# Attention, output projection and expert routing in three groups of three tiles, two of them inside the gather phase

## What is computed

```python
def fox_block(q, k, v, cq, ck, qpos, kpos):
    logits = jnp.einsum('bqhd,bkhd->bhqk', q, k).astype(F32) * (FOX_HD ** -0.5)
    logits = logits + (cq.transpose(0, 2, 1)[..., :, None] - ck.transpose(0, 2, 1)[..., None, :])
    logits = jnp.where((kpos[None, :] <= qpos[:, None])[None, None], logits, -jnp.inf)
    p = jax.nn.softmax(logits, axis=-1)
    return jnp.einsum('bhqk,bkhd->bqhd', p.astype(v.dtype), v)

def peer_tokens(x, wq, keys, u, v):
    q = jnp.einsum('nd,dc->nc', x, wq).reshape(n, PEER_HEADS, 2, PEER_HALF)
    s1 = jnp.einsum('nhd,hkd->nhk', q[:, :, 0], keys[0]).astype(F32)
    s2 = jnp.einsum('nhd,hkd->nhk', q[:, :, 1], keys[1]).astype(F32)
    v1, i1 = lax.top_k(s1, PEER_TOPK)
    v2, i2 = lax.top_k(s2, PEER_TOPK)
    cand = (v1[..., :, None] + v2[..., None, :]).reshape(n, PEER_HEADS, TOPK * TOPK)
    cv, ci = lax.top_k(cand, PEER_TOPK)          # and e: the expert numbers
    g = jax.nn.softmax(cv, axis=-1)
    act = jax.nn.gelu(jnp.einsum('nd,nhkd->nhk', x, u[e]).astype(F32))
    return jnp.einsum('nhk,nhkd->nd', g * act, v[e])

x = x + combine(ro, rg, fo, ret_out_g, fox_out_g, w_out, x.dtype)
x = x + peer(rms_norm(x, norm2_g), peer_wq, peer_keys, peer_u, peer_v)
```

## Time and profile before

| | us |
|---|---|
| median of three runs (4229.17 to 4239.43) | 4231.19 |
| the profiled execution | 4230.94 |
| its span, first to last instruction | 4229.1 |
| first attention scores | 690.00 |
| first gather issued | 1255.99 |
| first dot product | 1261.99 |
| VectorE, TensorE, ScalarE, POOL busy | 2474.3, 2507.5, 447.5, 1406.0 |
| mean DMA rate over the span | 305 GB/s |

### The profile page before, as it was taken

The page is one execution under the profiler, slowest core; times in us unless marked ns, Lnnn a source line. Parts: engine busy times, 40 slices in busy tenths (PEclk is TensorE's granted clock), DMA queues, the critical chain, the costliest instruction groups (busy, mean ns, idle before and its releaser), DMA issues.

```text
span 4229.1 us, 34501 instructions
## 1 busy us (share of the span) xinstructions
PE 2507.5 (59%) x11938; PEld 1040.8 (25%) x11938; DVE 2474.3 (59%) x6323; ACT 447.5 (11%) x1214; POOL 1406.0 (33%) x1276
## 2 busy tenths in 40 slices
PE   7998998998976336435435435534634634633333
PEld 3465444566432112101101101101201201201000
DVE  3211721331265875775785785685686686587555
ACT  1000112331110010000001001001001001001000
POOL 0000210000114444444444444444444444444443
PEclk9966997785997557767657767756756866856565
DMA  3001011002439999999999999999999999999999
GB/s 107 20 10 52 20 50 41 1 1 76 176 127 422 410 404 421 419 398 421 418 397 421 419 397 421 419 399 414 421 412 404 421 416 399 421 413 398 421 418 373
DMA packets 205134, 1289.95 MB, mean 305 GB/s; under 512 B 32024, under 2 KB 32856, under 8 KB 56352
## 3 DMA queue, kind: packets, MB, share of 16 engines
q0 software_dynamic: 165888, 1208.03, 69.0%
q1 hardware_dynamic: 36768, 77.40, 5.1%
q10 hardware_dynamic: 2304, 2.32, 0.2%
HBM read 1267.31 MB, written 20.09 MB: 304 GB/s over the span
## 4 chain that ended last, share of the span: by engine, by line
DMA 35%; PE 14%; DVE 12%; POOL 8%; issue 5%; ACT 1%; DVEq 0%; POOLq 0%
DMA mixo<-in_peer_uv,Xreg 16%; DMA Wreg<-in_peer_uv,Xreg 16%; PE yp L1370 11%; DMA spare<-in_peer_uv,Xreg 4%; POOL mixo L1165 3%; POOL Wreg L1165 3%; DVE Wreg L1442 2%; DVE mixo L1442 2%; PE spp L1409 1%; DVE strips L1472 1%; DVE Hreg L1566 1%; DVE Hreg L1563 1%; DVE Xreg L1569 1%; POOL spare L1165 1%; ACT gel L1243 1%
## 5 line engine op out<-in xcount | busy, mean ns | idle before, releaser
L1370 PE MATMUL yp<-Wreg,strips 128*32 128x512 f32 x2048 | 755.0, 991 | 736.0 <-DVE strips L1472 736.0
L1370 PE MATMUL yp<-mixo,strips 128*32 128x512 f32 x2048 | 751.6, 981 | 713.0 <-DVE strips L1472 713.0
L1442 DVE SCALAR_TENSOR_TENSOR Wreg<-Wreg,Hreg 128x1024 f32<-128x1024 f32 x512 | 626.8, 1225 | 363.3 <-DMA Wreg<-in_peer_uv,Xreg 358.5
L1165 POOL DMA_INDIRECT Wreg<-in_peer_uv,Xreg x512 | 585.0, 1143 | 736.2 <-PE yp L1370 600.2
L1442 DVE SCALAR_TENSOR_TENSOR mixo<-mixo,Hreg 128x1024 f32<-128x1024 f32 x512 | 626.5, 1224 | 347.1 <-DMA mixo<-in_peer_uv,Xreg 342.3
L1165 POOL DMA_INDIRECT mixo<-in_peer_uv,Xreg x512 | 586.1, 1145 | 728.9 <-PE yp L1370 607.8
L1370 PE MATMUL yp<-spare,strips 128*32 128x512 f32 x512 | 432.6, 996 | 174.3 <-DVE strips L1472 174.3
L323 PE MATMUL z<-Wreg,Hreg 128*128 128x512 f32 x1008 | 441.2, 594 | 1.4 <-PEq L105 1.1
L1370 PEld LDWEIGHTS yp<-Wreg,strips 128*32 128x32 f32 x2048 | 119.4, 150 | 1043.5 <-DVE strips L1472 865.7
L1370 PEld LDWEIGHTS yp<-mixo,strips 128*32 128x32 f32 x2048 | 119.4, 149 | 1021.7 <-DVE strips L1472 834.5
L1319 PE MATMUL qp<-Rreg,Hreg 128*128 128x512 f32 x576 | 289.2, 649 | 0.0
(11 more groups left out here) (226 smaller groups left out, 3035.2 us busy)
## 6 DMA issues: line engine op xcount, KB each, us to landing
Wreg<-in_w_in SPq DMA_DIRECT2D x7, 2048.0 KB, 9.2
Rreg<-in_peer_wq SPq DMA_DIRECT2D x8, 1024.0 KB, 21.1
Wreg<-in_peer_uv,Xreg POOLq DMA_INDIRECT x512, 10.1
mixo<-in_peer_uv,Xreg POOLq DMA_INDIRECT x512, 10.1
x_scratch<-Hreg SPq DMA_DIRECT2D x9, 512.0 KB, 2.6
xn_scratch<-mixo SPq DMA_DIRECT2D x9, 512.0 KB, 2.9
mixo<-x_scratch SPq DMA_DIRECT2D x9, 512.0 KB, 7.9
Rreg<-in_x_prompt SPq DMA_DIRECT2D x8, 512.0 KB, 6.1
```

Source lines behind the costliest of these rows:

```text
L1165: nc.gpsimd.indirect_dma_start(ring[n % NR], None, uv_tab, bass.IndirectOffsetOnAxis(ap=idxH[:, t % 2, s // 4, s % 4:s % 4 + 1], axis=0)). ...
L1370: last = nc.tensor.matmul(yp[32 * j:32 * j + 32, 512 * c:512 * c + 512], strips[:, n % 2, j, :], ring[(4 * n + j) % NR][:, D + 512 * c:D + ...
L1442: nc.vector.scalar_tensor_tensor(out=row, in0=row, scalar=1.0, in1=xrep[:, s % 4, :], op0=ALU.mult, op1=ALU.mult, accum_out=dots[:, t % 2, ...
```

## The change

The two phases become one, `phase_tail`. The nine tiles are three groups of three (`GROUPS`, `GT`). `front_steps(g)` lists all steps of attention, output projection and routing for a group, with an estimated TensorE and VectorE time each; group 2 has two prompt tiles and the sample tile. Group 0's list runs ahead of the gather loop on every engine. `due_steps` spreads the lists of groups 1 and 2 over the 96 rounds of the three tiles before them (a round is one k: four gathers). In the loop each engine does its part of the steps due in a round: TensorE, ScalarE and POOL ahead of the round's own work, VectorE between its dots.

```diff
+        def due_steps():
+            due = [[] for _ in range(32 * TILES)]
+            for g in range(1, GROUPS):
+                pe_us, dve_us, at = 0.0, 0.0, []
+                for s in front_steps(g):
+                    at.append(max(pe_us / 6.0, dve_us / 3.2))
+                    pe_us, dve_us = pe_us + s[0], dve_us + s[1]
+                stretch = (32 * GT - 7) / at[-1]
+                for s, b in zip(front_steps(g), at):
+                    due[32 * GT * (g - 1) + int(b * stretch)].append(s[2:])
+            return due
...
+                for step in front_steps(0):
+                    front(step[2:])
+                pool.wait_ge(q_mm, 4 * GT)
+                for n in range(NR):
+                    gather(n)
+                for b in range(32 * TILES):
+                    for step in due[b]:
+                        front(step)
+                    for n in range(4 * b + NR, min(4 * b + NR + 4, P * TILES)):
+                        gather(n)
...
                 for t in range(TILES):
-                    coming = route(t + 1) if t + 1 < TILES else iter(())
                     for s in range(P):
                         dot(t, s)
+                        for step in between(due[32 * t + s // 4], s % 4):
+                            front(step)
                         if s % 4 == 3:
                             weigh(t, s // 4)
-                        if s >= ROUTE_S and (s % 4 < 3 or s % 8 == 3):
-                            next(coming, None)
...
-        program(phase_fox)
-        program(phase_peer)
+        program(phase_tail)
```

More of the change, by code:

```diff
@@ new lines, in front @@
+                def front(step):
+                    kind, g = step[0], step[1]
+                    if kind == "hpow":
+                        pool.wait_ge(hs_done, GT * g + GT)
+                        rsqrt(0, 24, 1.0 / HD)
+                        for i in range(GT):
+                            last = nc.gpsimd.tensor_tensor(small[:, 24 + 8 * i:32 + 8 * i], small[:, 24 + 8 * i:32 + 8 * i],
+                                                           nhalf[:, :], ALU.pow)
+                        last.then_inc(rs_done, 1)
+                    elif kind == "hpow2":
+                        pool.wait_ge(xsq, GT * g + GT)
+                        rsqrt(48, GT, 1.0 / D)
+                        nc.gpsimd.tensor_tensor(small[:, 51:54], small[:, 51:54], nhalf[:, 0:GT], ALU.pow).then_inc(xrs, 1)
@@ L1188, in _ @@
-                pool.wait_ge(y_mm, TILES)
-                for i in range(2):
-                    pool.wait_ge(xn_out[i], 16 * (5 - i))
-                for t in range(TILES):
-                    pool.wait_ge(moved, 16 * (t + 1))
-                    for s in range(P):
-                        gather(t, s)
+                nc.gpsimd.memset(ones0, 1.0).then_inc(ones_set, 1)
+                for step in front_steps(0):
+                    front(step[2:])
+                pool.wait_ge(q_mm, 4 * GT)
@@ L1301, in _ @@
+                        for step in due[32 * t + k]:
+                            front(step)
+                        if k == 31 and t + 1 < TILES:
+                            for j in range(3):
+                                spread_x(t + 1, j)
+                        gelu_tanh(32 * t + k)
+                    if t + 1 < TILES:
                         spread_x(t + 1, 3)
@@ new lines, in turn_probs @@
+                def turn_probs(n, second):
+                    g, h, t = FOX[n]
+                    pe.wait_ge(exp_done, n + 1)
+                    if second:
+                        claim("C", ptb, WIDE[n + 1])
+                    else:
+                        claim("C", pta, n + 1)
+                    for j in range(4, t + 1) if second else range(min(4, t + 1)):
+                        last = nc.tensor.transpose(four(C)[:, j % 4, :], pr[:, n % 3, j * P:(j + 1) * P], ident[:, :])
+                    last.then_inc(tb_mm if second else ta_mm, 1)
@@ new lines, in values @@
+                def values(n):
+                    g, h, t = FOX[n]
+                    b0 = 64 * (h % 2)
+                    pe.wait_ge(pta, n + 1)
+                    pe.wait_ge(ptb, WIDE[n + 1])
+                    claim("D", ov_ev, n + 1)
+                    for j in range(t + 1):
+                        last = nc.tensor.matmul(Dk[b0:b0 + 64, 0:P], vg[:, j, h * HD:(h + 1) * HD], pT[:, n % 2, j, :],
+                                                start=(j == 0), stop=(j == t))
+                    last.then_inc(pv_done, 1)
@@ new lines, in fox_bank @@
+                def fox_bank(n):
+                    return AB[:, :] if FOX[n][2] >= 4 else half_ab[n % 2]
+                def replicate_x(t, j):
+                    if j == 0:
+                        pe.wait_ge(xTn_in, 16 * (t + 1))
+                    for half in range(2):
+                        piece = 8 * t + 2 * j + half
+                        if piece >= 2:
+                            pe.wait_ge(xr_ev, piece - 1)
+                        for k in range(4):
+                            for b in range(4):
+                                last = nc.tensor.matmul(EF[32 * b:32 * b + 32, half, k * P:(k + 1) * P],
+                                                        xTn[:, 4 * half + k, 32 * j:32 * j + 32], ident[:, :],
+                                                        start=True, stop=True)
+                        last.then_inc(rep_mm, 1)
@@ new lines, in dot @@
+                def dot(t, s):
+                    n = t * P + s
+                    dve.wait_ge(uv_in[n % NR], 16 * (n // NR) + 16)
+                    if s < 4:
+                        dve.wait_ge(xr_ev, 8 * t + 2 * s + 2)
+                    row = ring[n % NR][:, 0:D]
+                    nc.vector.scalar_tensor_tensor(out=row, in0=row, scalar=1.0, in1=xrep[:, s % 4, :],
+                                                   op0=ALU.mult, op1=ALU.mult,
+                                                   accum_out=dots[:, t % 2, s:s + 1]).then_inc(dot_done, 1)
@@ L1640, in _ @@
                         if s == 2 and t >= 1:
                             finish(t - 1)
-                        if t + 1 < TILES and s == 4 * GATE_K + 1:
-                            for _ in coming:
-                                pass
-                            gates(t + 1)
                 finish(TILES - 1)
```

1575 lines of the change are left out of this document (806 added, 769 removed).

## The result

The changed kernel takes 4366.24 us (median of four runs, 4360.62 to 4370.94) against 4235.28 for the kernel before in the same comparison: a ratio of 1.0309, 95% interval 1.0291 to 1.0328. The prediction said 4216 with a range of 4160 to 4310. The profiled execution has a span of 4369.0 against 4229.1.

What follows compares the result with a forecast made beforehand. It saw a 1256 us front on TensorE and VectorE, then a DMA-bound gather phase. Span 4229.1 - 193 (earlier start) + 147 (bytes) + 31 (losses) = 4214, forecast 4216 us, range 4160 to 4310.

Steps and rivals of the forecast that it cites:

- Earlier start: Front: only tiles 0 to 2 processed before gathering, first dot product at 1073, 193 us earlier, bounds 165 to 220.
- More bytes: Gather phase: groups 1 and 2 move 63.7 MB, 58.2 MB of it paid in full on busy DMA, 147 us.
- Losses inside the gather phase: Gather rounds: DMA time lost to added attention, projection and routing steps, 85 us against 54 today, +31.
- the prediction's sign: Gather phase: DMA share 1.00 except in the sample tile's fourteen rounds, where VectorE waits for TensorE's values.
- the sample tile's rounds: Cached attention in fourteen gather rounds: rounds stretch up to 19 us, 37 us lost, bounds 15 and 60.
- The alternative: Cached attention's clock: if busy time counted as activity, `add_v` and scores would halve, the sum falling by 17 us.
- Prompt attention: Gather rounds of groups 1 and 2: attention on TensorE plus `add_v` costs 13 us, bounds 0 and 110.
- The powers on POOL: Gather phase: two power steps per group stand between gathers in POOL's queue, VectorE waits, 5 us.
- Rival 1: Gather rounds break under prompt attention as VectorE's score reduction waits for TensorE: 4308 us, chance 0.23.
- Rival 4: Group 1's routing late for tile 3, so gathers stop: a round or two, 20 us, chance 0.02.

Runs made afterwards that it cites:

- e8: e7 with group 0's first two query-weight blocks loaded after attention, with x, not ahead of the third decay row; 4164.23 us, 0.9844 of the kernel before.
- e4: e1 with w_out and query weights of groups 1 and 2 loaded twice, 25.2 MB more; 4356.13 us, 1.0283 of the kernel before.
- e1: Changed kernel with the candidate-choice pieces spread over the rounds left instead of bunched in two rounds; 4279.03 us, 1.0128 of the kernel before.
- e3: e1 with the candidate choice of tiles 1 and 2 moved behind the first dot product; 4254.89 us, 1.0077 of the kernel before.
- e6: e1 with empty steps between loads and their users, and neither table clock lagging over a round; 4258.24 us, 1.0049 of the kernel before.
- e7: e3 with e6's leads, more empty steps, slightly fewer rounds, and K and V loaded separately earlier; 4183.66 us, 0.9868 of the kernel before.

## Why the prediction was wrong, step by step

Its sum was 4229.1 - 193 + 147 + 31 = 4214; the span is 4369.0, 155 more. With what each term measured it is 4229.1 - 159 + 162 + 133 = 4365, which leaves 4 us unexplained. (One side figure of the prediction was a slip: without the 147 us for bytes the sum is 4067, not 4071.)

*Earlier start: mechanism right, 34 us short.* The first dot product stands at 1105.38, predicted 1073 and "wrong outside 1045 to 1100". Attention began at 696.58 and not 690, at the bound of +8 given for scan, store and read-back; its matmuls ran at PEclk 0.51 in the mean, the low level at which they were mostly priced, with the 9 us hole that e8 explains: end 778 instead of 765. Projection and norm took 78 us and not 70; the twelve blocks 123 (122 said), the last top 16 took 7 and not 5. Choosing took 36.8 us a tile and not 35, from 986 to 1096.6, and then 8.8 us for indices, gates and x where 6 was said. The tenth gather followed 14 us later (1119.31) and not 12. No single step of it failed; eight small ones leaned the same way, and in the prediction's own reckoning (a stream begun 22.4 us ahead of the tenth gather) the start came 1256 - 1097 = 159 us earlier, just outside the bounds of 165 to 220.

*More bytes: the bytes right, the term 15 us short.* The table's 53 MB more hide that nine gathers (9.4 MB) had landed before its count begins in the changed kernel. From the tenth gather on, 1272 MB moved; less 1143 gathers and the 13.6 MB of x1, xn and y are 60 MB of the groups' own traffic, where 58.2 was said. At the 416.9 GB/s of this kernel's full stretches they take 144 us (147 said). What the prediction did not have is that full stretches ran at 419.5 GB/s before and 416.9 after, 18 us on the 1222 MB of before: together 162 us, at its upper bound. Why the rate fell was not taken apart. e4 confirms the price of a byte by doubling. The rule that the prediction cites from the Trainium skill (DMA: Bandwidth & Descriptors, section "Issuing engines are not separate DMA queues"), that DMAs issued by different engines share the sixteen, agrees with e4: 66 us for 25.2 MB.

*Losses inside the gather phase: here it failed.* Predicted 85, measured 189 from the first dot product and 183 from the tenth gather. The step was: "The routing operations are cut into halves of about 1.15 us, two or three a round". That is true of rounds 64 to 88 and 169 to 184, but 47 + 64 of the 198 pieces stand in two rounds, worth 136 us. The prediction took a mean over the rounds left instead of reading the table at the point where one engine's sum stops growing. The table itself was at hand and has those 47 pieces in one round; the profile of before could not show it, but the cost would have followed (35 us of choosing a tile by the prediction, a ring of 22 us). Without the 136 the losses are 47 to 53, less than 85. So the prediction's sign, DMA share below 1.00 only in the sample tile's rounds, also failed: the two holes lie outside them.

The other terms in it: the sample tile's rounds were priced at 37 us, measured 246 x 0.05 = 12, half of it the wait for the first cached keys. The mechanism is there, VectorE waits for the values in each such round, as in

```profile
2520.08 0.48 DVE L1614 COPY M<-d 64x64 f32<-64x64 f32 x2 [4.39 <-PE d L1343]
```

but from one `weigh` to the next a round with a request took 12 to 15.5 us, one of them 19.5, where 17 to 19 was said: from the score reduction at 2515.25 to the next at 2529.95 it is 14.7. The term was mis-sized mainly by the clock: the granted clock in these rounds was 0.67 in the mean and not the 0.50 of the earlier trace rows, and in one request the same four values matmuls stand at both levels:

```profile
2515.98 0.63 PE L1341 MATMUL d<-M 128*128 128x32 f32 x4
...
2516.88 1.06 PE L1341 MATMUL d<-M 128*128 128x32 f32 x4
```

The alternative that the prediction puts beside the Trainium skill (TensorE: Matmul & The Clock Gate, section "What's actually happening"), the sum lower by 17, would have come nearer; how the level comes about no run here shows. Prompt attention, priced at 13, cost about nothing: 1206 to 1306 has a share of 1.01 at PEclk 0.81. The powers on POOL and the steps around them: TensorE waits 11.75 us for them in group 1, where the stretch 1369 to 1450 is at 0.94: 5 us, as priced for both groups together. Group 2 has such a wait of 13.18 us as well, within the sample tile's stretch counted above, so the term was somewhat small. What I had not named at all, a TensorE wait for a load with the round's own work behind it, cost some 11 us here (half of it within the sample tile's 12) and became the main new loss in e1 and e3.

*The rivals.* Rival 1 (rounds break under prompt attention, 4308) had the sign and the nearest number, for a reason that the trace refutes; that it came nearest was luck. Rival 4 asked whether routing would come late; it did not. That the table of rounds could have a lump was none of them. The range ended at 4310 and the chance of slower was 0.36.

## What to carry to other kernels

When a table spreads work over rounds by max(sum of A, sum of B), look at every place where the work turns from A-heavy to B-only: there all of B's pieces fall due at once. Count the instructions per round of the engine that frees the buffers in the order itself, not in the mean; here a round of L us cost about L less its usual 10. And in an in-order queue a step needs its loads several rounds ahead when DMA is full: with the lump gone, leads of three to four rounds for keys and caches went with 1.0049 instead of 1.0128 in e6, and, with K and V loaded much earlier too, 0.9868 instead of 1.0077 in e7. A front that looks idle may already be prefetching: e3's 72.5 us gave 22. The idea of the change was sound: with lump and leads mended it is 1.3 to 1.6% faster than before.

## What the runs showed of the hardware

With DMA engines full of gathers, loads took long to land: in the changed kernel the keys' pieces of 256 KB 20.7 us in the median of all twelve from issue to landing, w_out's of 512 KB 22.6 and the query weights' of 2 MB 28.5 (front and gather phase together). Their users waited up to 26.33 and 31.21 us for K, V and Q in e3 (1.5 and 2 MB each for K and V) and 17.61 for keys in e1; in the changed kernel the user of keys issued at 1535.66 started at 1573.12. By contrast, in the front, with a DMA share of 0.26 over 856 to 868, keys issued at 856.55 held up nothing at 867.98. TensorE's clock: in group 0's attention it was granted 0.50 (the 1.2 GHz level) over 720 to 750 with TensorE busy 27.26 of 30 us, and in group 0's queries 1.00 (2.4 GHz) over 880 to 920, busy 34.59 of 40:

```profile
720.00:750.00 30.00, 27.26 (x87) 15.28 (x87) 5.66 (x25) 11.01 (x39) 0.00 (x0) 0.50 0.10 21
...
880.00:920.00 40.00, 34.59 (x113) 16.95 (x112) 22.19 (x128) 7.02 (x12) 0.00 (x0) 1.00 0.02 7
```

In these stretches the busier one had the lower level: the busy share of a stretch does not tell its level.
